# Chunked delta rule in a one-core kernel: one decay matrix for both triangles, and three steps placed half a weight unit later

## The reference, cut to what matters

```
cum_g = jnp.cumsum(gc, axis=-1)
decay = jnp.exp(jnp.where(causal, cum_g[..., :, None] - cum_g[..., None, :], -jnp.inf))
m = jnp.where(strict, jnp.einsum("nbhid,nbhjd->nbhij", kb, kc) * decay, 0.0)
t = lax.linalg.triangular_solve(eye + m, ..., lower=True, unit_diagonal=True)
u = t @ (vc * bc)
w = t @ (kb * jnp.exp(cum_g)[..., None])
qk = jnp.einsum("nbhid,nbhjd->nbhij", qc, kc) * decay
```

## Time and profile before

| | us |
|---|---|
| median of 3 runs (2912.35 to 2914.92) | 2912.67 |
| the profiled execution, its own time | 2914.45 |
| its span, first to last instruction | 2912.7 |
| PE busy in the span | 2877.0 (99%) |
| DVE busy | 1911.3 (66%) |
| ACT busy | 1425.5 (49%) |
| the delta rule's stage, begin to end | about 1081 to 1745 |

### The profile page before, as it was taken

One profiled execution on the slowest core, in us unless ns is written; L12 is line 12 of the kernel. 1 busy time (PEld: TensorE's weight loads), 2 busy tenths in 40 slices (PEclk: granted clock), 3 DMA queues, 4 the chain that ended last, 5 costly groups with the idle time before them and its releaser, 6 DMA issues.

```text
span 2912.7 us, 39284 instructions
## 1 busy us (share of the span) xinstructions
PE 2877.0 (99%) x16096; PEld 2495.3 (86%) x16096; DVE 1911.3 (66%) x2441; ACT 1425.5 (49%) x1816; POOL 51.6 (2%) x101
## 2 busy tenths in 40 slices
PE   9999999999999999999999999999999999999998
PEld 8899888888888888888888888888888888888886
DVE  7645567678656567778878765456656555556555
ACT  5334653456444456666666643534345434444444
POOL 0000200000000000000000000000000000000000
PEclk9999999999999999999999999999999999999999
DMA  7444345565554544343333445544355454554543
GB/s 281 182 174 159 145 160 202 188 240 181 179 203 168 194 163 154 121 145 131 131 134 128 144 156 193 186 188 159 135 193 194 174 202 178 199 199 177 190 186 145
DMA packets 73139, 506.81 MB, mean 174 GB/s; under 512 B 8416, under 2 KB 8544, under 8 KB 13184
## 3 DMA queue, kind: packets, MB, share of 16 engines
q1 hardware_dynamic: 71568, 498.21, 46.4%
q0 software_dynamic: 1104, 5.90, 0.6%
q10 hardware_dynamic: 288, 0.18, 0.0%
HBM read 500.07 MB, written 2.10 MB: 172 GB/s over the span
## 4 chain that ended last, share of the span: by engine, by line
PE 90%; DVE 5%; ACT 3%; issue 1%; DMA 1%; SPq 0%; ACTq 0%; DVEq 0%; POOL 0%
PE double L1285 82%; PE bank L1285 6%; PE bank L1288 1%; DVE cacc L2013 1%; DVE wlo L2007 1%; ACT whi L1661 1%; DVE cst L2030 0%; ACT L1878 0%; DVE Mn L2013 0%; DMA vec<-in_vec 0%; DMA raw<-in_wall 0%; DVE cst L2007 0%; ACT tmp L1857 0%; DVE cacc L2010 0%; DVE Mo L2007 0%
## 5 line engine op out<-in xcount | busy, mean ns | idle before, releaser
L1285 PE MATMUL double<-AA,whi 128*128 128x512 f32 (+1 forms) x5008 | 1657.8, 383 | 4.9 <-DVE wlo L2007 4.3
L1285 PE MATMUL double<-AA,wlo 128*128 128x256 f32 (+1 forms) x4624 | 1301.1, 281 | 0.0
L1661 ACT ACTIVATE whi<-raw 128x1024 fp32r<-128x1024 f32 x926 | 924.8, 1048 | 724.2 <-PE double L1285 695.7
L2007 DVE TENSOR_TENSOR wlo<-raw,whi 128x1024 fp32r<-128x1024 f32 (+1 forms) x934 | 1102.1, 1213 | 231.8 <-ACT whi L1661 229.8
L1285 PEld LDWEIGHTS double<-AA,whi 128*128 128x128 f32 x5008 | 915.9, 188 | 194.1 <-DVE wlo L2007 5.8
L1285 PEld LDWEIGHTS double<-AA,wlo 128*128 128x128 f32 x4624 | 871.4, 188 | 1.4
L1285 PE MATMUL double<-whi,AA 128*128 128x512 f32 x1536 | 492.1, 394 | 0.5 <-DVE wlo L2007 0.5
L1285 PEld LDWEIGHTS double<-whi,AA 128*128 128x128 f32 x1536 | 289.2, 188 | 60.8 <-DVE wlo L2007 1.3
L1285 PE MATMUL double<-whi,BB 128*128 128x512 f32 x1024 | 316.9, 389 | 0.0
L1285 PE MATMUL double<-wlo,AA 128*128 128x512 f32 x768 | 299.7, 390 | 0.0
L1285 PEld LDWEIGHTS double<-whi,BB 128*128 128x128 f32 x1024 | 192.2, 188 | 40.3
(11 more groups left out here) (336 smaller groups left out, 1878.5 us busy)
## 6 DMA issues: line engine op xcount, KB each, us to landing
raw<-in_wall SPq DMA_DIRECT2D x462, 1024.0 KB, 4.8
raw<-in_wall SPq DMA_DIRECT2D x9, 256.0 KB, 6.8
X<-in_xT SPq DMA_DIRECT2D x1, 2048.0 KB, 11.2
Mm<-in_memT POOLq DMA_DIRECT2D x1, 2048.0 KB, 15.2
tmp<-rqk POOLq DMA_DIRECT2D x16, 128.0 KB, 2.2
mblk<-in_memT SPq DMA_DIRECT2D x8, 256.0 KB, 6.8
out<-XT SPq DMA_DIRECT2D x8, 256.0 KB, 2.9
dec<-in_dec POOLq DMA_DIRECT2D x1, 1536.0 KB, 8.3
```

What stands on the lines that cost most here:

```text
L1285: return q.matmul(out, lhsT, rhs, start=start, stop=stop, skip_group_check=True)
L1661: q.activation(whi[j % SPL][:, c], raw[j % RAW][:, c], ACT.Copy).then_inc(S("w_hi"), 1)
L2007: return q.tensor_tensor(out, a, b, o)
```

## The change: what it does

In g_dec DVE now forms `dM` and then, in one instruction, the smaller of `dM` and `-dM`; ACT takes one Exp of that into `dE`, which serves both triangles. `dC` is computed after it, and DVE no longer waits for `dC`. In g_mat the whole product `Mf` = k k^T times beta times `dE` is formed by four instructions, then `Mn` by masking it; the block between the chunks is read from `Mf` by g_up64, so `Mo` and its two instructions are gone. Three more `yield`s are put in: before g_inv0 (in round 0 there were two extra ones already, of which one stays extra), before g_up of d = 2, and before g_tr. ACT loads one table set that holds both Ln and Exp ahead of the norms' `rsqrt` and of g_dec.

```
     def g_gdn(h):
...
-        side.free(b1, "gdn_vec", r["a1"])
+        side.free(b1, "gdn_act", r["e"])
         side.held.add(b2)
         yield
...
         side.free(b3, "gdn_vec", r["w"])
         yield
+        yield
         if h == 0:
-            yield
             yield
         b1, f1 = side.take()
         r = add("g_inv0", h, b1=b1, f1=f1, p1=up("gdn_pe"), c=up("gdn_vec", 2), x=up("gdn_vec"), xd=up("gdn_act", 2))
         side.free(b1, "gdn_vec", r["c"])
         x, xd = r["x"], r["xd"]
+        yield
         yield
         for d in (2, 4, 8, 16, 32):
...
         add("g_end", h, v=up("gdn_vec", 4))
+        yield
         yield
         b1, f1 = side.take()
         r = add("g_tr", h, b=b1, bf=f1, p=up("gdn_pe"), m=up("gdn_m"))
...
         def s_cvn(key, r):
+            q.preload_act_table_set("natural_log_exp_and_others")
             q.wait_ge(S("cnv_pe"), r["full"])
...
         def s_g_dec(h, r):
-            if h:
-                q.wait_ge(S("gdn_vec"), at["g_x", h - 1]["y"])
-            else:
+            if not h:
                 q.wait_ge(S("gab_act"), at["gab2", 0]["a"])
-            q.wait_ge(S("gdn_pe"), r["p1"])
+            q.preload_act_table_set("natural_log_exp_and_others")
+            q.wait_ge(S("gdn_vec"), r["a2"])
+            q.activation(f2(dE), f2(dM), ACT.Exp).then_inc(S("gdn_act"), 1)
             for g in range(2):
                 row = bank[r["b1"]][:, (2 * g + 1) * 128:(2 * g + 2) * 128]
                 q.activation(dC[:, g, :], row, ACT.Exp, bias=rest[:, 2 * h + g:2 * h + g + 1]).then_inc(S("gdn_act"), 1)
-            q.wait_ge(S("gdn_vec"), r["a3"])
-            q.activation(f2(dM), f2(dM), ACT.Exp).then_inc(S("gdn_act"), 1)
-            q.activation(f2(dU), f2(dU), ACT.Exp, scale=-1.0).then_inc(S("gdn_act"), 1)
...
-            q.wait_ge(S("gdn_act"), r["e"])
+                q.wait_ge(S("gdn_act"), at["g_dec", h - 1]["x"])
+            q.wait_ge(S("gdn_pe"), r["p1"])
             tt(four(dM[:, :, :]), col(cum, h), four(bk(r["b1"])), ALU.subtract).then_inc(S("gdn_vec"), 1)
             q.wait_ge(S("gdn_vec"), r["a1"])
-            ts1(f2(dU), f2(dM), 0.0, ALU.max).then_inc(S("gdn_vec"), 1)
-            q.wait_ge(S("gdn_vec"), r["a2"])
-            ts1(f2(dM), f2(dM), 0.0, ALU.min).then_inc(S("gdn_vec"), 1)
+            stt(f2(dM), f2(dM), -1.0, f2(dM), ALU.mult, ALU.min).then_inc(S("gdn_vec"), 1)
...
-            tt(Mn[s][:, :, :], dM[:, :, :], bc("strict"), ALU.mult).then_inc(S("gdn_vec"), 1)
...
-                stt(Mn[s][:, k, :], bk(r["b2"])[:, k, :], b, Mn[s][:, k, :], ALU.mult, ALU.mult).then_inc(S("gdn_vec"), 1)
-            below = Mo[s][LATE, :, 0:64]
-            tt(below, bk(r["b2"])[LATE, :, 0:64], dM[LATE, :, 0:64], ALU.mult).then_inc(S("gdn_vec"), 1)
-            q.wait_ge(S("gdn_vec"), r["o1"])
-            tt(four(below), four(below), col_late(beta, h), ALU.mult).then_inc(S("gdn_vec"), 1)
+                stt(Mf[s][:, k, :], bk(r["b2"])[:, k, :], b, dE[:, k, :], ALU.mult, ALU.mult).then_inc(S("gdn_vec"), 1)
+            q.wait_ge(S("gdn_vec"), r["o"])
+            tt(Mn[s][:, :, :], Mf[s][:, :, :], bc("strict"), ALU.mult).then_inc(S("gdn_vec"), 1)
             q.wait_ge(S("gdn_pe"), r["p3"])
-            tt(qkt[s][:, :, :], bk(r["b3"]), dU[:, :, :], ALU.mult).then_inc(S("gdn_vec"), 1)
+            tt(qkt[s][:, :, :], bk(r["b3"]), dE[:, :, :], ALU.mult).then_inc(S("gdn_vec"), 1)
```

More of the change, by code:

```diff
@@ L798, in g_gdn @@
         b2, f2 = side.take()
-        r = add("g_dec", h, b1=b1, f1=f1, b2=b2, f2=f2, p1=up("gdn_pe"), p2=up("gdn_pe"), e=up("gdn_act", 2),
-                a1=up("gdn_vec"), a2=up("gdn_vec"), a3=up("gdn_vec"), x4=up("gdn_act"), x5=up("gdn_act"))
-        side.free(b1, "gdn_vec", r["a1"])
+        r = add("g_dec", h, b1=b1, f1=f1, b2=b2, f2=f2, p1=up("gdn_pe"), p2=up("gdn_pe"), a1=up("gdn_vec"), a2=up("gdn_vec"),
+                x=up("gdn_act"), e=up("gdn_act", 2))
+        side.free(b1, "gdn_act", r["e"])
         side.held.add(b2)
@@ L804, in g_gdn @@
         b3, f3 = side.take()
-        r = add("g_mat", h, b2=b2, b3=b3, f3=f3, p3=up("gdn_pe"), a4=up("gdn_vec"), m=up("gdn_vec", 4), o1=up("gdn_vec"), o=up("gdn_vec"),
-                w=up("gdn_vec"))
-        side.free(b2, "gdn_vec", r["o1"])
+        r = add("g_mat", h, b2=b2, b3=b3, f3=f3, p3=up("gdn_pe"), o=up("gdn_vec", 4), m=up("gdn_vec"), w=up("gdn_vec"))
+        side.free(b2, "gdn_vec", r["o"])
         side.free(b3, "gdn_vec", r["w"])
         yield
+        yield
         if h == 0:
-            yield
             yield
@@ L1161, in program @@
     qkv = [block(kpos, "qkv" + x) for x in "qkv"]
-    dM, dU, dC = block(kpos, "dM"), block(kpos, "dU"), block(kpos, "dC")
-    names = ("cross", "vb", "Mo", "qkt", "Mn", "TT")
+    dM, dE, dC = block(kpos, "dM"), block(kpos, "dE"), block(kpos, "dC")
+    names = ("cross", "vb", "Mf", "qkt", "Mn", "TT")
     set0 = [block(vpos, n + "_0") for n in names]
@@ L1168, in program @@
     set1 = [ar.get([P_, 4, 128], name=n + "_1") for n in names]
-    cross, vb, Mo, qkt, Mn, TT_ = [list(x) for x in zip(set0, set1)]
+    cross, vb, Mf, qkt, Mn, TT_ = [list(x) for x in zip(set0, set1)]
     rest_at = ar.off
@@ L1240, in col @@
         return x[:, :, 2 * h:2 * h + 2].rearrange("p t h -> p h t").unsqueeze(3).broadcast_to([P_, 2, 2, 128])
-    def col_late(x, h):
-        return x[LATE, :, 2 * h:2 * h + 2].rearrange("p t h -> p h t").unsqueeze(3).broadcast_to([64, 2, 2, 64])
     def X2(j):
@@ L1542, in s_g_up64 @@
             for k in range(4):
-                ins = mm_group(bank[r["b1"]][EARLY, k * 64:(k + 1) * 64], Mo[s][LATE, k, 0:64], Tc[LATE, k, :])
+                ins = mm_group(bank[r["b1"]][EARLY, k * 64:(k + 1) * 64], Mf[s][LATE, k, EARLY], Tc[LATE, k, :])
             ins.then_inc(S("gdn_pe"), 1)
@@ L2508, in s_g_mat @@
                 q.wait_ge(S("gdn_pe"), at["g_o", (h - 2, 1)]["p"])
-            q.wait_ge(S("gdn_act"), at["g_dec", h]["x5"])
-            tt(Mn[s][:, :, :], dM[:, :, :], bc("strict"), ALU.mult).then_inc(S("gdn_vec"), 1)
+            q.wait_ge(S("gdn_act"), at["g_dec", h]["x"])
             q.wait_ge(S("gdn_pe"), at["g_dec", h]["p2"])
-            q.wait_ge(S("gdn_vec"), r["a4"])
             for k in range(4):
                 b = beta[:, k % 2, 2 * h + k // 2:2 * h + k // 2 + 1]
-                stt(Mn[s][:, k, :], bk(r["b2"])[:, k, :], b, Mn[s][:, k, :], ALU.mult, ALU.mult).then_inc(S("gdn_vec"), 1)
-            below = Mo[s][LATE, :, 0:64]
-            tt(below, bk(r["b2"])[LATE, :, 0:64], dM[LATE, :, 0:64], ALU.mult).then_inc(S("gdn_vec"), 1)
-            q.wait_ge(S("gdn_vec"), r["o1"])
-            tt(four(below), four(below), col_late(beta, h), ALU.mult).then_inc(S("gdn_vec"), 1)
+                stt(Mf[s][:, k, :], bk(r["b2"])[:, k, :], b, dE[:, k, :], ALU.mult, ALU.mult).then_inc(S("gdn_vec"), 1)
+            q.wait_ge(S("gdn_vec"), r["o"])
+            tt(Mn[s][:, :, :], Mf[s][:, :, :], bc("strict"), ALU.mult).then_inc(S("gdn_vec"), 1)
             q.wait_ge(S("gdn_pe"), r["p3"])
-            tt(qkt[s][:, :, :], bk(r["b3"]), dU[:, :, :], ALU.mult).then_inc(S("gdn_vec"), 1)
+            tt(qkt[s][:, :, :], bk(r["b3"]), dE[:, :, :], ALU.mult).then_inc(S("gdn_vec"), 1)
         def s_g_inv0(h, r):
@@ L2799, in s_load_mb @@
         def s_load_mb(n, r):
-            name, value = (("cnv_vec", at["cv1", (7, 2)]["v"]), ("cnv_vec", at["cvv", 7]["z"]), ("gdn_vec", at["g_mat", 7]["o1"]),
+            name, value = (("cnv_vec", at["cv1", (7, 2)]["v"]), ("cnv_vec", at["cvv", 7]["z"]), ("gdn_act", at["g_dec", 7]["x"]),
                            ("gdn_vec", at["g_mat", 7]["w"]), ("gdn_pe", at["g_x", 7]["p"]), ("gdn_pe", at["g_vb", 7]["p"]),
```

1 line of the change is left out of this document (removed).

## The result

| | before | after |
|---|---|---|
| median of 4 runs each, us | 2913.39 (2912.35 to 2914.92) | 2896.9 (2895.17 to 2899.32) |
| ratio, 95% interval | | 0.9945 [0.9932, 0.9957] |
| the profiled execution, its own time | 2914.45 | 2899.32 |
| its span | 2912.7 | 2897.5 |

The change gains 16.5 us by the medians and 15.2 by the spans of the two profiled executions. The forecast was 11.1 us, and its range ended at 2899.0: faster, as forecast, but by more than the range allowed. All these gains are under 1% of the time, and the interval of each ratio lies clear of 1.

What follows compares the result with a forecast made beforehand. PE, busy 2877.0 of 2912.7 us, was taken to bound the kernel. Of its waits 15.3 us go and 4.2 come back, 11.1 gained: 2912.7 - 11.1 = 2901.6 us, range 2899 to 2907.5.

Steps and rivals of the forecast that it cites:

- What bounds the kernel: PE, busy 2877.0 of 2912.7 us; its waits in the delta rule's stage give 15.3 us to act on.
- I take 5.2, as it stands alone in the queue: Mk phase: block 5's load, issued after g_vb of round 7, lands in 5.2 us, from a traced 5.2 to 7.2.
- it waits 4.2 us: Mk phase: PE waits 4.2 us (4.1 to 6.2) for block 5 and the columns after it; 4.9 of waits before.
- Rival E: Mk phase: block 5 lands by PE's arrival, only 1.85 us of wait left; 13.4 us gained, 2899.3 us, chance 0.05.
- The wait for `cacc_r` ... nothing in front of it changes, and it stays: Convolution ahead of the first g_dec: PE's wait for `cacc_r` is unchanged, so no gain there.
- The same price on both sides, so no term: Mk phase: half clock for 3.4 us after PE's wait, 1.7 us lost both before and after the change.
- I cost it at nothing: Rounds: three DVE instructions and one Exp fewer each, 16 table loads fewer in all, hidden beside PE's work: 0 us.
- the half step ahead of g_up: 4.8: The `yield` before g_up, d = 2, removes six `Tc` waits of rounds 1 to 6, 4.8 us; round 7's 1.1 too.
- The half steps for `Mn` and `ob`: The `yield` before g_inv0 removes four `Mn` waits, 4.8 us; that before g_tr removes three `ob` waits, 1.8 us.
- the shorter chain: Round 1: Exp follows the table load sooner, so `Mn` is ready at about 1200.5, 4 us early.
- Rivals A to D: A: longer load wait, 2905.3, 0.09; B: `Tc` stays late, 2906.1, 0.08; C: `wlo` waits, 2912.7, 0.13; D: late `U`, 2924.4, 0.07.

Runs made afterwards that it cites:

- the experiment with the block there long before: Changed kernel with the places of blocks 5 and 6 exchanged, so block 5 needs only g_x of round 7: 2896.88 us.
- the table set alone: Kernel before with only the one table set for the norms, 16 table loads fewer on ACT: 2910.89 us against 2912.09, ratio 0.9998.
- half steps alone: Kernel before with only the three added `yield`s, its own matrices and table loads kept: 2900.97 us against 2912.09.
- the mathematics alone: Changed kernel without its three added `yield`s, keeping `dE`, `Mf` and the one table set: 2899.57 us, 12.5 gained on the kernel before.
- the columns behind `Tc`: Changed kernel with columns 8 to 11 of `AA` placed behind g_down, d = 2, so DVE has `Tc` first: 2896.26 us.
- the last version: Changed kernel with columns 8 to 11 and 12 to 15 of `AA` later and Sigmoid's table loaded before the `cacc` wait: 2891.84 us, second run 2893.01.

## Why the prediction was wrong

*What bounds the kernel: right.* Time regained on PE was regained at the end. 15.3 us of waits, each its idle time plus 0.16, was what the change acted on, and all of it went.

*"I take 5.2, as it stands alone in the queue": the step that failed.* The 5.2 came from the earlier trace rows, and every load there had a load of `raw` in front of it, issued 0.4 to 3.3 us earlier. SP's timeline of the kernel before has:

```profile
1669.43 9.96 SPq L2781 DMA_DIRECT2D raw<-in_wall  x2
1679.43 0.91 SPq L2804 DMA_DIRECT2D mblk<-in_memT  x2
1685.18 0.33 SPq L2781 DMA_DIRECT2D raw<-in_wall  x1
```

The second load of the first row went out at 1679.06, and the six of the earlier trace rows follow on the last row. So the landing times told of the queue in front, not of the blocks' own 256 KB. Block 5 with nothing in front takes 2.9 to 3.0 us in the three profiles of the changed kernel, and 5.1 behind `raw` in the experiment that moved only its load. The term "it waits 4.2 us" measured 2.2, 2.0 too much. The layout around it was right: block 5 issued behind g_vb, two columns and `Tc` behind the landing in 1.93 us (1.85 forecast), PE arriving 3.0 us after g_vb's end (2.85). With this term alone put right the forecast would have been about 2899.6, still 2.7 above the measured median: what is said below of `cacc_r` and of the clock was needed too.

*Rival E had the landing.* It asked for a landing by the time PE arrives, and gave 2899.3 with its chance of 0.05. Its 1.85 us of remaining wait came near the 2.04 measured, but in part by luck: it counted them from the landing, and the experiment with the block there long before still had 1.80. What holds PE then is ACT, which comes to the four columns only behind `whi`, and DVE, which has them ahead of `Tc`. The estimate of 2.6 us worked out from the Trainium skill's page "DMA: Bandwidth & Descriptors", section "Anatomy of one DMA — SWDGE (gpsimd) path", is 0.3 under the 2.9 measured; I set it aside for a row that measured something else. The Trainium skill's section "Queues, rings and completion order" on that page states that each DMA engine takes descriptors in ring order, and the 5.1 us behind `raw` agrees.

*"The wait for `cacc_r` ... nothing in front of it changes, and it stays": wrong.* The norm of q stands in front of it, and lost a table load. 0.5 us by the waits, shown by the table set alone.

*"The same price on both sides, so no term": wrong in its reason.* The prediction counts one of the two stretches at half clock in the kernel before. Behind `cacc_r` one was there at waits of 1.75, 1.56 and 1.5 us (before, half steps alone, `dC` behind the Exps), missing at about 1.3 in eight profiles, and missing at 1.5 in the third profile of the changed kernel. Behind `Tc` of the mk phase the changed kernel had it at 2.04 and 2.11 and not at 2.09. It is no fixed cost of a wait: it comes in some executions and not in others; in the profiled pair it is worth 1.7 us.

*"I cost it at nothing" (the mathematics): right in the sum, wrong in what it says.* Beside the half steps it adds little in the rounds, since they remove the same waits. Alone it brings 12.5 us. I had read `Mn`'s chain in the timeline but not what DVE waited for at its start (3.44 us, for `dC`), nor that `Cm` and `Tc` had no idle time in front of them. From these two the common cause could have been seen, and "the half step ahead of g_up: 4.8" would not have stood there as a term of its own.

*The half steps for `Mn` and `ob`: right in size.* For `Mn` the alternative in the same paragraph, the shorter chain, turned out enough by itself. `ob` needed its half step: with the mathematics alone its 1.2 us stayed.

*Rivals A to D.* No wait for `wlo` came up in the stage, and none for `U` that the view of waits lists (PE's product on `U` at 1654.41 started 0.13 us after the modelled end of the one ahead of it, once in the eight rounds). One stretch at half clock and not two stood near 1700, and the half-us waits for `Tc` were gone.

*The sum, mended.* 15.3 - 2.2 + 0.5 = 13.6 us by the waits and 1.7 by the clock. The three differences of medians are 16.5, 17.2 and 16.2. The 1 to 2 us over 15.3 stay open, but the profiles show what differs from one execution to the next. Both stretches at half clock can be present before and absent after, which is worth up to 3.4. The load at the start differs by about 1.0 us between two profiles of the changed kernel. And there is a slow stretch far behind the change, where PE never stands still and the granted clock is full. Over 90 us that begin 20 us behind the same product, the first and the second profile of the changed kernel have:

```profile
2087.80:2177.80 90.00, 90.00 (x509) 1.00 0.50 187
...
2086.90:2176.90 90.00, 90.00 (x519) 1.00 0.52 195
```

Ten products fewer at 0.17 us each are 1.7 us. The profiles of the kernel before, of the columns behind `Tc` and of the second run of the last version also have 509 or 510 there, the other nine 519. So in the pair that the result compares it is on both sides and cancels, and elsewhere it need not. What makes it, no run here shows.

## What to carry to other kernels

Before a wait is priced, look at what its releaser stood idle for: `Tc` was late because DVE's queue was, and DVE was late because of a value (`dC`) that it did not need yet. Letting DVE form `dM` without that value, with one pair of steps exchanged on ACT, brings 10.9 us where the whole change brings 16 to 17. Two edits aimed at one cause do not add up, so price them together. And take the duration of a load from a row with the same queue in front of it.

## What the runs showed of the hardware

- The time to landing of a 256 KB load from SP hung on what had been issued just before. Over the 14 profiles it was 2.7 to 3.2 us with nothing issued in the 3 us ahead, and 5.0 to 7.9 with 1 MB issued 0.4 us ahead; in the kernel before the last of six behind such a load took 7.2.
- PE's clock dropped to 0.50 for 3.4 us behind waits of 1.5 to 2.1 us in some executions, and not in others of the same kernel; at the wait of 6.4 us it was at 0.50 for 6.8 us, from 2 us before the wait ended. Two profiles, of the half steps alone and of the columns behind `Tc`, show one such stretch some 26 us after the start, behind waits for `wlo` of 1.8 us (the changed kernel's first profile has such a wait of 1.8 us there too, and no stretch); the second has none at all behind its later waits.
- An ACT_TABLE_LOAD took 1283 ns in every group of lines, and loaded ahead of a wait it was free: `cacc_r` lost its whole wait of 1.28.
- In one and the same 90 us of unbroken products at a granted clock of 1.00, PE ran 509 or 510 products in four of 14 profiles and 519 in the others: 1.7 us.
